# Shared weights, norm tables and down weights asked for elsewhere, and three rows instead of four for VectorE, in a mixture-of-experts step on one Trainium2 core

## The reference

```
h = x * (1 + scale) + shift                       # per kind of token, from the condition
w, idx = top-8 of 64 sigmoid scores, group-limited, normalised, times 2.5
f(h)   = sum over the 8 chosen experts of w_e * (silu(h @ wg_e) * (h @ wu_e)) @ wd_e
         + (silu(h @ sg) * (h @ su)) @ sd         # the shared expert
x      = LayerNorm(ALPHA * x + gate * f(h)) * g + b
```

## Time and profile before

| | |
|---|---|
| median of 3 runs | 1925.76 us (1922.42 to 1932.57) |
| the profiled execution | 1924.23 us, its span 1922.8 us |
| granted TensorE clock, mean | 0.92 |
| busy: PE, DVE, ACT, POOL | 84%, 34%, 18%, 17% |
| DMA | 590.23 MB, 307 GB/s over the span |
| routing, experts, combine of layer 0 | from about 367, 391, 990 us |
| of layer 1 | from about 1244, 1268, 1865 us |

### The profile page before, as it was taken

How to read it: one execution, slowest core, us unless ns; L and a number is a source line. 1 busy time by engine, 2 the same in 40 slices (tenths; PEclk the granted TensorE clock), 3 DMA queues, 4 the chain that set the end, 5 groups by cost and what they waited for, 6 DMA issues and landing times. The chain is left out here.

```text
span 1922.8 us, 19140 instructions
## 1 busy us (share of the span) xinstructions
PE 1613.6 (84%) x6824; PEld 786.6 (41%) x6824; DVE 646.8 (34%) x1355; ACT 347.1 (18%) x761; POOL 318.8 (17%) x248
## 2 busy tenths in 40 slices
PE   4997777589999589889966989679999778888866
PEld 1564533444444233333323854444444333333322
DVE  2233746643221011111128874753131111111117
ACT  2214610111111011111112163011111111111120
POOL 0010014012111122332101401202111123111100
PEclk8999988699999889989987999789999989999988
DMA  9871093479999999999956022188999999999965
GB/s 390 335 285 56 23 349 123 175 291 359 408 413 404 417 405 407 389 401 398 385 240 258 6 88 94 68 333 319 409 401 398 413 399 404 399 403 378 380 255 221
DMA packets 113538, 590.23 MB, mean 307 GB/s; under 512 B 23240, under 2 KB 25288, under 8 KB 55712
## 3 DMA queue, kind: packets, MB, share of 16 engines
q1 hardware_dynamic: 88864, 535.45, 69.1%
q0 software_dynamic: 24000, 50.48, 6.8%
q10 hardware_dynamic: 576, 3.03, 0.4%
HBM read 576.14 MB, written 48.40 MB: 325 GB/s over the span
## 5 line engine op out<-in xcount | busy, mean ns | idle before, releaser
L2459 PE MATMUL bank<-weights,scratch 128*64 128x512 f32 x448 | 224.1, 659 | 88.5 <-DMA scratch<-in_moe_w_up 45.1
L2564 DVE TENSOR_TENSOR scratch<-scratch,bank 128x256 f32<-128x256 f32 x88 | 53.9, 613 | 676.1 <-ACT scratch L2533 647.3
L2460 PE MATMUL bank<-scratch 128*64 128x512 f32 x480 | 234.3, 645 | 0.0
L2459 PEld LDWEIGHTS bank<-weights,scratch 128*64 128x64 f32 x448 | 65.7, 152 | 236.6 <-issue 236.6
L2533 ACT ACTIVATE scratch<-bank 128x256 f32<-128x256 f32 x88 | 33.8, 384 | 711.1 <-PE bank L2460 433.5
L2459 PE MATMUL bank<-scratch 128*64 128x512 f32 x288 | 131.7, 612 | 17.3 <-DMA scratch<-in_moe_w_up 17.3
L2465 PE MATMUL bank<-weights,scratch 128*128 128x512 f32 x320 | 141.9, 596 | 3.0 <-ACT scratch L2528 1.7
L2460 PE MATMUL bank<-weights,scratch 128*64 128x512 f32 x256 | 122.1, 633 | 0.0
L2265 POOL DMA_INDIRECT y_rows<-hP,y_idx x42 | 43.3, 1030 | 464.3 <-DVE hP L2569 392.3
L2465 PE MATMUL bank<-scratch 128*128 128x512 f32 x256 | 112.9, 594 | 0.0
L2260 POOL DMA_INDIRECT hP<-h_rows,tok_idx x82 | 86.4, 1054 | 144.1 <-PE bank L2221 81.7
(11 more groups left out here) (367 smaller groups left out, 2529.2 us busy)
## 6 DMA issues: line engine op xcount, KB each, us to landing
weights<-in_moe_w_gate SPq DMA_DIRECT2D x64, 1024.0 KB, 11.8
weights<-in_moe_w_up SPq DMA_DIRECT2D x64, 1024.0 KB, 17.8
weights<-in_moe_w_down SPq DMA_DIRECT2D x64, 1024.0 KB, 20.7
scratch<-in_moe_w_gate SPq DMA_DIRECT2D x64, 1024.0 KB, 11.7
scratch<-in_moe_w_up SPq DMA_DIRECT2D x64, 1024.0 KB, 21.0
scratch<-in_moe_w_down SPq DMA_DIRECT2D x64, 1024.0 KB, 18.0
weights<-in_w_mod SPq DMA_DIRECT2D x6, 2048.0 KB, 11.3
wmod_more<-in_w_mod SPq DMA_DIRECT2D x6, 2048.0 KB, 8.8
```

Of the source, the lines that this page charges most:

```text
L2459: nc.tensor.matmul(out[0:HALF, :], x[:, 0:HALF], w0[:, kk], start=(kk == 0), stop=(kk == KT - 1))
L2460: m = nc.tensor.matmul(out[HALF:P, :], x[:, HALF:P], w1[:, kk], start=(kk == 0), stop=(kk == KT - 1))
L2564: nc.vector.tensor_tensor(B.h[b % 2].rearrange("p (j q) -> p q j", j=2), B.ex[b % 2].rearrange("p (q j) -> p q j", j=2), k.ps[2 + b % 2][: ...
```

## The change

1. A fifth weight buffer at the head, in z, used once by expert number 4; later experts use the four (`slot_of`, `user_before`, `loads_of`). The shared weights go to z afterwards, asked for by SP behind routed block 7 (`SHARED_LOAD`), and the shared blocks become blocks 11, 20 and 29.
2. Down weights from expert number 5 on are asked for by ACT, on ACT's own DMA queue, in `finish`, behind its copy. SP issues only gate and up, and the down loads of experts 3 and 4.
3. The combine's tables are loaded behind all weights (`combine_tables`), when the down product two blocks from the end is done. Only ln1's g and b stay at routed block 18. Layer 0's folding of g and b is done in the routing stage, on rows spread over 16 partitions (`FoldRows`), with the result in DRAM (folded_rows), from where it is broadcast.
4. In the combine VectorE adds rows 0, 2, 4 and TensorE the other five. The norm is two steps on VectorE, of which the first doesn't wait for the reciprocal root; in layer 0 the normed x itself is written by ACT.

`load_norm_tables` now serves the mixer's norm alone.

```diff
+def combine_tables(k, eng, layer):
+
+    M = NormBuffers(k, 2)
+
+    def load(out, row):
+        eng.dma_start(out, row.to_broadcast([P, D])).then_inc(k.s_ahead[4], 16)
+        k.ahead[4] += 16
+
+    for cnd in range(2):
+        load(M.T[:, cnd, 0, :], k.mod_d[layer, cnd:cnd + 1, 5 * D:6 * D])
+        if layer + 1 < DEPTH:
             for j in range(2):
-                at = (layer, 3 + j) if which == 1 else (layer + 1, j)
-                table_load(k, eng, s_tab, M.T[:, cnd, 1 + j, :], at[0], cnd, at[1])
+                load(M.T[:, cnd, 1 + j, :], k.fold_d[cnd, j:j + 1, :])
+    if layer + 1 == DEPTH:
+        for j, n in enumerate("gb"):
+            load(M.gb[:, j, :], k.io[f"ln2_{n}"][layer:layer + 1, :])
...
+class FoldRows:
...
+    def load(self, k, eng, layer, sem):
+        for c in range(2):
+            eng.dma_start(self.all[self.rows(c), 0:2, :], self.across(k.mod_d[layer + 1, c, 0:2 * D])).then_inc(sem, 16)
+            for j, n in enumerate("gb"):
+                eng.dma_start(self.all[self.rows(c), 2 + j:3 + j, :], self.across(k.io[f"ln2_{n}"][layer, :])).then_inc(sem, 16)
+
+    def store(self, k, eng, sem):
+        for c in range(2):
+            eng.dma_start(k.fold_d[c].rearrange("j (p n) -> p j n", p=8), self.all[self.rows(c), 0:2, :]).then_inc(sem, 16)
+
+    def steps(self, eng):
+        tt = eng.tensor_tensor
+        shift, scale, g, b = self.shift, self.scale, self.g, self.b
+        return [lambda: tt(shift, shift, b, ALU.add), lambda: tt(b, b, scale, ALU.mult), lambda: tt(shift, shift, b, ALU.add),
+                lambda: tt(scale, scale, g, ALU.mult), lambda: tt(scale, scale, g, ALU.add)]
...
         @blk.sync
         def _(sp):
-            w = shared_views(k)
-            k.load_ahead(sp, 3, w[0], io["shared_w_gate"][layer].rearrange("(p k) n -> p (k n)", k=KT))
-            k.load_ahead(sp, 3, w[1], io["shared_w_up"][layer].rearrange("(p k) n -> p (k n)", k=KT))
-            k.load_ahead(sp, 3, w[2], io["shared_w_down"][layer].rearrange("(p j) n -> p (j n)", j=2))
-
+            if folds:
+                F.load(k, sp, layer, s_fl)
             for e in range(FIXED):
                 sem = k.s_ahead[FIXED_SEM[e]]
                 load_expert(k, sp, layer, e, e, sem, sem)
                 k.ahead[FIXED_SEM[e]] += 48
+                if folds and e == 0:
+                    sp.wait_ge(s_fs, 5)
+                    F.store(k, sp, s_fd)
+            if folds:
+                sp.wait_ge(s_fd, 32)
 
         @blk.gpsimd
         def _(pool):
 
             nc.gpsimd.memset(k.hP[:], 0.0)
+            if folds:
+                pool.wait_ge(s_fl, 16 * 6)
+                for i, step in enumerate(F.steps(nc.gpsimd)):
+                    if i:
+                        pool.wait_ge(s_fs, i)
+                    step().then_inc(s_fs, 1)
...
+def slot_of(i):
+
+    return i if i <= WSLOTS else (i - 1) % WSLOTS
+
+
+def user_before(i):
+
+    users = [j for j in range(i) if slot_of(j) == slot_of(i)]
+    return users[-1] if users else None
+
+
+def loads_of(i):
+
+    return len([j for j in range(FIXED, i + 1) if slot_of(j) == slot_of(i)])
+
+
 def expert_views(k, b):
-    w = k.ring[:, b * 6144:(b + 1) * 6144] if b < 2 else k.s[:, 2816 + (b - 2) * 6144:2816 + (b - 1) * 6144]
+    w = (k.z[:, 0:6144] if b == WSLOTS else k.ring[:, b * 6144:(b + 1) * 6144] if b < 2
+         else k.s[:, 2816 + (b - 2) * 6144:2816 + (b - 1) * 6144])
...
-SHARED_AFTER = (0, 8, 13)
+SHARED_AFTER = (11, 19, 27)
+SHARED_LOAD = 7
...
     def on_sync(sp):
-        def down(i, e):
-            if i >= WSLOTS:
-                sp.wait_ge(s_d, block_of[i - WSLOTS] + 1)
-            load_down(k, sp, layer, e, i % WSLOTS, s_wd[i % WSLOTS])
-
-        waiting = []
         for b in routed[FIXED:]:
             _, at, ranks = plan[b]
-            block = []
             for i in range(at, at + len(ranks)):
                 e = sp.value_load(k.perm[0:1, rank_at[i]:rank_at[i] + 1], min_val=0, max_val=NE - 1)
-                if i >= WSLOTS:
-                    sp.wait_ge(s_gu, block_of[i - WSLOTS] + 1)
-                load_gate_up(k, sp, layer, e, i % WSLOTS, s_wg[i % WSLOTS])
-                block.append((i, e))
-            for i, e in waiting:
-                down(i, e)
-            waiting = block
+                if user_before(i) is not None:
+                    sp.wait_ge(s_gu, block_of[user_before(i)] + 1)
+                load_gate_up(k, sp, layer, e, slot_of(i), s_wg[slot_of(i)])
+                if user_before(i) is None:
+                    load_down(k, sp, layer, e, slot_of(i), s_wd[slot_of(i)])
+            if order[b] == SHARED_LOAD:
+                sp.wait_ge(s_gu, block_of[WSLOTS] + 1)
+                load_shared(k, sp, layer, "gate_up")
+                sp.wait_ge(s_d, block_of[WSLOTS] + 1)
+                load_shared(k, sp, layer, "down")
             if order[b] == FOLD_FROM - 1:
                 sp.wait_ge(s_done, 1)
-                sp.wait_ge(s_d, last_shared + 1)
-                load_norm_tables(k, sp, layer, 2, k.s_ahead[3], k.s_ahead[3])
                 for j, name in enumerate(("ln1_g", "ln1_b")):
-                    sp.dma_start(spare[:, (j + 1) * D:(j + 2) * D], k.io[name][layer:layer + 1, :].to_broadcast([P, D])).then_inc(k.s_ahead[3], 16)
-                k.ahead[3] += 16 * (6 if last_layer else 10)
-        for i, e in waiting:
-            down(i, e)
+                    k.load_ahead(sp, 3, ln1[:, j * D:(j + 1) * D], k.io[name][layer:layer + 1, :].to_broadcast([P, D]))
+        sp.wait_ge(s_d, max(last_shared, block_of[user_before(NE - 1)]) + 1)
+        combine_tables(k, sp, layer)
...
         count(0)
+        turn_rows(0)
         for b in range(N):
...
         def finish(b):
             finish_wait(act, b)
             nc.scalar.copy(y_out(b, slice(0, 512)), k.ps[5][:]).then_inc(s_ya, 1)
-
+            for i in range(NE):
+                if user_before(i) is not None and block_of[user_before(i)] == b:
+                    e = act.value_load(k.perm[0:1, rank_at[i]:rank_at[i] + 1], min_val=0, max_val=NE - 1)
+                    act.wait_ge(s_d, b + 1)
+                    load_down(k, act, layer, e, slot_of(i), s_wd[slot_of(i)])
+
+        copy_x(0)
         for b in range(N):
...
+DVE_ROWS = (0, 2, 4)
+PE_ROWS = tuple(j for j in range(TOPK) if j not in DVE_ROWS)
...
     def on_tensor(pe):
         for t in range(TILES):
             pe.wait_ge(s_dg, t + 1)
-            for j in range(half):
-                pe.wait_ge(s_g[2 * t + (2 * j + 1) // half], 16)
+            for i, j in enumerate(PE_ROWS):
+                pe.wait_ge(s_g[2 * t + j // half], 16)
                 for c in range(2):
-                    m = nc.tensor.matmul(k.ps[2 * t + c][:], diag[:, t, j, :], y_row(t, 2 * j + 1)[:, c * 512:(c + 1) * 512],
-                                         start=(j == 0), stop=False)
+                    m = nc.tensor.matmul(k.ps[2 * t + c][:], diag[:, t, i, :], y_row(t, j)[:, c * 512:(c + 1) * 512],
+                                         start=(i == 0), stop=False)
                 m.then_inc(s_pacc, 1)
-            pe.wait_ge(s_acc, half * (t + 1))
+            pe.wait_ge(s_acc, ND * (t + 1))
...
     def on_scalar(act):
         for t in range(TILES):
-            for j in range(half):
-                m = nc.scalar.mul(diag[:, t, j, :], k.ident, k.w8[:, t, 2 * j + 1:2 * j + 2])
+            for i, j in enumerate(PE_ROWS):
+                m = nc.scalar.mul(diag[:, t, i, :], k.ident, k.w8[:, t, j:j + 1])
             m.then_inc(s_dg, 1)
         for t in range(0 if last else TILES):
+            x = k.x[:, t, :]
+            act.wait_ge(s_nb, t + 1)
+            nc.scalar.activation(x, x, ACT.Identity, bias=M.nb[:, t:t + 1], scale=M.mv[:, t, 1:2])
             copy_turned(k, act, t, turn_banks[t], s_tr)
...
         def norm(t):
+            x = k.x[:, t, :]
+            mu, rstd = M.mv[:, t, 0:1], M.mv[:, t, 1:2]
+            G, B, out = (M.gb[:, 0, :], M.gb[:, 1, :], x) if last else (M.T[:, min(t, 1), 2, :], M.T[:, min(t, 1), 1, :], k.hP[:, t, :])
+            st.then(nc.vector.scalar_tensor_tensor(out, x, mu, G, ALU.subtract, ALU.mult))
+            dve.wait_ge(s_p, t + 1)
+            nc.vector.scalar_tensor_tensor(out, out, rstd, B, ALU.mult, ALU.add).then_inc(s_h, 1)
             if not last:
-                dve_norm(k, M, dve, st, t, s_p, s_n, s_h, False)
-                return
-            x = k.x[:, t, :]
-            dve.wait_ge(s_p, t + 1)
-            st.then(nc.vector.tensor_scalar(x, x, M.mv[:, t, 0:1], M.mv[:, t, 1:2], ALU.subtract, ALU.mult))
-            st.then(nc.vector.tensor_tensor(x, x, M.gb[:, 0, :], ALU.mult))
-            nc.vector.tensor_tensor(x, x, M.gb[:, 1, :], ALU.add).then_inc(s_h, 1)
+                nc.vector.tensor_scalar(M.nb[:, t:t + 1], mu, rstd, -1.0, ALU.mult, ALU.mult).then_inc(s_nb, 1)
```

(49 more changed lines are left out.)

50 lines of the change are left out of this document (32 added, 18 removed).

## The result

The changed kernel takes 1934.27 us in the median (1927.69 to 1939.60, 13 runs) beside 1926.66 us of the kernel before (1921.86 to 1932.57, 13 runs): ratio 1.0036 [1.0022, 1.0051], 6.9 us slower. The forecast was 25 us faster.

What follows compares the result with a forecast made beforehand. Each layer: a TensorE-bound head, a long rest bound by weights' DMA, a VectorE-bound combine. Layer 0 -10 - 3 + 1 - 3 = -15, layer 1 -5 - 3 + 1 - 3 = -10: 1924.2 - 25 = 1899 us; range 1880 to 1919.

Steps and rivals of the forecast that it cites:

- The queue: Down loads on ACT's queue: taken as 0, range -8 to +12 us a layer, since buffers waited for products, not issues.
- Rival (a): Down loads on ACT's queue push gate/up loads back in 13 windows: 49 us, 1948 us in all; 8 in 100.
- among two-expert blocks 12 us stand there: Argument against the push-back rival: 12 us of loads stand behind the needed one; it decides only under 5 us.
- the sign named for (a): If down loads push gate/up loads back, gate/up landings grow and windows under DMA share 0.95 multiply.
- The 30.6 us of waits for weights: Second layer: TensorE stands at gate/up products for weights 9 times, 30.6 us; first layer said to look the same.
- The head: Start of each layer's expert stretch: fifth buffer and later shared weights cut DMA idle, 3 us a layer gained.
- each of the first five blocks releases one expert's place: Head: 9.0 us of DMA against 11.7 of TensorE, so 2.7 us idle each, 13.5 us.
- nearly paid for by the shared weights, which are the same bytes, later: Head: the fifth buffer's extra expert load is nearly offset by shared weights loaded later; head gain taken as 3 us a layer.
- begins at the same time: Head: without the shared block as filler, the first expert waits for the same rows and still begins at 404.40.
- the shared blocks cost nothing in their late places: Shared blocks at 11, 20 and 29: zero cost, with 6 us kept for the range.
- The tables: Broadcast tables leave the weights' stream: 10.0 us gained in layer 0, 5.0 in layer 1; tail cost +1 a layer.
- The combine: End of each layer: one row less and a shorter norm on VectorE, less TensorE's delay: 3 us gained a layer.

Runs made afterwards that it cites:

- the tail's runs: Last seven experts' down loads back on SP: in the kernel before plus ACT queue 1923.09 us, changed kernel with head undone 1908.49, changed kernel whole 1920.45.
- the queue with its tail mended: Kernel before with down loads moved to ACT's queue, except the last seven experts' per layer, which SP asks for: 1923.09 us, 0.9983.
- the kernel with the new head: Changed kernel with fifth buffer and late shared blocks kept, only the last seven experts' down loads put back on SP: 1920.45 us, 0.9964.

## Why the prediction was wrong

Between the forecast (-25) and the result (+6.9) lie 31.9 us. By the kernels above 19.8 of them are the queue's, 7.7 the head's (-6 forecast, +1.7 without the queue), 1.9 the tables' and 2.5 the combine's.

**The queue: the step that failed.** The forecast took 0, between -8 and +12 us a layer; it measured +14.3 alone and +19.8 with the head, so up to 10 a layer, within the bound but at the end taken for unlikely. The step that failed is the reading that order is worth nothing because the buffers wait for products. Rival (a) had the mechanism: overtaking. Its price of 49 us counted 13 stretches of mid-stage, where by the tail's runs overtaking costs nothing unless the new head stands beside it (6.0 us are left then). It missed the one place without cover, the end of the stream; the argument against it ("among two-expert blocks 12 us stand there") holds for mid-stage and fails exactly there. SP's 228.6 us at the down loads were no loss: their removal is worth the 3.3 us of the queue with its tail mended (3.9 beside tables and combine). That wait held the loads in the order in which TensorE needs them. In after, landings of layer 1 from 1340 to 1850 are, for down loads, gathers and gate/up loads:

```profile
DMA to landing us min/median/max: 7.9/10.7/16.3
...
DMA to landing us min/median/max: 9.0/12.9/16.3
...
DMA to landing us min/median/max: 4.8/15.1/32.7
```

Before they were 19.6, 10.7 and 15.2 us in the median. Down loads, needed last, got a share of their own and came sooner. Gate/up loads came no later in the median, so the sign named for (a) shows at the tail only (22.9 us for 16.9). The 30.6 us of waits for weights that the prediction read from the earlier trace rows were 54.2 in all; no term of its sum used them.

The Trainium skill (page DMA: Bandwidth & Descriptors, section Issuing engines are not separate DMA queues) gives a second issuer its issue time and no more. The -3.3 us with the order kept at the tail agree; the +14.3 us of the queue alone don't, since the rule leaves out the order. The Trainium skill (page DMA: Bandwidth & Descriptors, section Queues, rings and completion order) says that a DMA engine takes its queues in turn. The landings above agree.

**The head: wrong sign beside the queue.** The count that "each of the first five blocks releases one expert's place" and "nearly paid for by the shared weights, which are the same bytes, later" overlooked that the block with two small experts releases two places with four buffers, and that the fifth place waits 25 us for its load. In those 25 us the kernel with the new head moved 304 GB/s and the kernel before 354: 1.25 MB, 3.0 us, as much as the head was to gain in a layer. Why it costs more than that beside the queue is open. That the first product loses a filler and "begins at the same time" was right on the start (11.3 us after the gather, before 12.4), but not on its length. Without the shared block TensorE was idle ahead of it, the granted clock of 390 to 400 us was 0.50 where it was 0.66 and that of 400 to 410 us 0.81 where it was 1.00. The product took 8.82 us for 7.11, at half clock in part, and ended 20.1 us after the gather's issue, before 19.5. That the shared blocks cost nothing in their late places was right as far as it can be told (late against first: 0.9893 to 0.9904); the windows show that not any place would do.

**The tables: right.** 10.0 and 5.0 us were forecast for their bytes, 10.0 and 4.9 measured at the last up load, closer than two profiles can tell. In layer 1 some 3 us return in the tail (38.8 us from last up load to y_rows before, 42.0 with late tables), where +1 was taken. The folding in the routing stage cost nothing that shows: first gather 25.1 us after the stage's start before, 25.1 after.

**The combine: right in kind, half in size.** The timeline of layer 1's combine in after, beside the earlier trace rows:

```profile
1880.16 11.30 PE L2856 MATMUL bank<-scratch 128*128 128x512 f32 x20 [15.20 <-DMA scratch<-y_rows]
...
1897.67 4.06 DVE L2888 SCALAR_TENSOR_TENSOR cat<-weights,w,cat 128x1024 f32<-128x1024 f32 x3
...
1901.65 1.28 DVE L2910 SCALAR_TENSOR_TENSOR x_tok<-x_tok,z,hT 128x1024 f32<-128x1024 f32 x1
1902.97 1.28 DVE L2912 SCALAR_TENSOR_TENSOR x_tok<-x_tok,z,hT 128x1024 f32<-128x1024 f32 x1
```

Three rows take 4.06 us for 5.46, the norm 2.56 for 3.25, the first tile's products 11.30 for 9.83 (1.5 us more, where 1.7 to 2.5 was forecast). From the loads of y_rows to the end it is 55.9 us for 57.9, 2 us and not 3; other profiles scatter by about 1 us. In layer 0 the last copy comes 2.3 us sooner, but the next stage starts 2.0 us later behind it, in all kernels with this combine; why is open.

**The range** ended at 1919 because (a) was left out of it with 8 in 100. Its upper bound of the queue part (+12 a layer, 24 us) would have given 1923 by the forecast's own sum, and did not enter either.

## What to carry to other kernels

A wait in an issuing engine's program that costs nothing may be what keeps transfers in the order of need: before loads move to a queue of their own, write down which load the next product needs and what can now pass it, and look at the end of the stream first, where nothing is left to cover it. If the second queue is wanted, leave the last few loads on the first. A new buffer is worth what it holds: follow each place from release to next issue, and count the time in which it stands empty.

## What was not expected of the hardware

In these runs two queues with full work share the engines by queue and not by age: with the down loads on a second queue their median from issue to landing fell from 19.6 to 10.7 us, while a load of the first queue that had waited 5 us longer came 7 us later, and gathers on the third went from 10.7 to 12.9 us. DMA's busy share doesn't show what is moved: 445 to 470 us had a share of 0.88 at 304 GB/s in the kernel with the new head, and the same stretch of the one with four buffers and late blocks 0.96 at 375, so the gap in bytes (19%) was more than twice that in share (8%).
